# A two-block transformer kernel whose modulation sums move: from the third vector on, one multiply-and-add of VectorE per tile instead of column sums and transposes

## The reference, cut to what matters

```python
c_act = jax.nn.silu(c)                      # [1, 1024]
mod = c_act @ w_ada[l] + b_ada[l]           # w_ada: [1024, 6144]
sh1, sc1, g1, sh2, sc2, g2 = split(mod, 6)
h = rmsnorm(x, norm1_g) * (1.0 + sc1) + sh1
... attention and pooling of h, projected by w_out ...
x = x + g1 * mix
h2 = rmsnorm(x, norm2_g) * (1.0 + sc2) + sh2
x = x + g2 * conv_gated_ffn(h2, ...)
```

## Time and profile before

| | |
|---|---|
| median of 3 runs | 1458.22 us (1455.87 to 1458.29) |
| the profiled execution | 1456.54 us, of it a span of 1454.7 us |
| TensorE busy | 1401.7 us (96% of the span) |
| VectorE busy | 828.4 us (57%) |
| ScalarE busy | 649.5 us (45%) |
| GpSimd busy | 703.7 us (48%) |
| granted TensorE clock, mean | 0.985 of full speed |

### The profile page before, as it was taken

The page is one execution under the profiler, slowest core; times in us unless marked ns, Lnnn a source line. Parts: engine busy times, 40 slices in busy tenths (PEclk is TensorE's granted clock), DMA queues, the critical chain, the costliest instruction groups (busy, mean ns, idle before and its releaser), DMA issues.

```text
span 1454.7 us, 18428 instructions
## 1 busy us (share of the span) xinstructions
PE 1401.7 (96%) x7351; PEld 1181.1 (81%) x7351; DVE 828.4 (57%) x1289; ACT 649.5 (45%) x1199; POOL 703.7 (48%) x380
## 2 busy tenths in 40 slices
PE   7889989999999999999999999999999999999998
PEld 6668778988888888987778877788889888888886
DVE  5567746668888675656777976552357421302224
ACT  4455536444332331544776765456454331323231
POOL 1246554365555454554333454338815654545560
PEclk7799999999999999999999999999999999999999
DMA  8314523255555454321111211113211222232321
GB/s 320 141 65 161 175 103 114 102 209 172 187 198 201 177 202 153 124 87 59 59 59 59 87 59 58 59 58 134 98 59 59 87 87 87 90 113 88 111 92 58
DMA packets 32053, 167.59 MB, mean 115 GB/s; under 512 B 3552, under 2 KB 4192, under 8 KB 18912
## 3 DMA queue, kind: packets, MB, share of 16 engines
q1 hardware_dynamic: 31968, 166.42, 32.4%
HBM read 164.31 MB, written 2.10 MB: 114 GB/s over the span
## 4 chain that ended last, share of the span: by engine, by line
PE 84%; DVE 7%; ACT 4%; POOL 2%; issue 1%; DMA 1%; SPq 0%; DVEq 0%; ACTq 0%
PE B L552 81%; PE B L974 1%; POOL WL L2327 1%; ACT WH L1195 1%; DVE SC L1950 1%; PE B L784 1%; DVE SC L2178 1%; DMA RAW<-in_x 1%; DVE ZF L2153 1%; PE B L667 1%; POOL G L2365 0%; DVE M L2151 0%; DVE ZF L2133 0%; PE B L690 0%; DVE ZF L1861 0%
## 5 line engine op out<-in xcount | busy, mean ns | idle before, releaser
L2327 POOL TENSOR_TENSOR WL<-RAW,WH 128x512 fp32r<-128x512 f32 (+1 forms) x197 | 467.9, 2390 | 499.3 <-ACT WH L1195 453.7
L552 PE MATMUL B<-HH,WH 128*128 128x512 f32 (+2 forms) x1040 | 404.5, 391 | 5.9 <-ACT HH L1281 2.1
L552 PE MATMUL B<-HH,WL 128*128 128x512 f32 (+2 forms) x1040 | 397.2, 384 | 0.0
L552 PE MATMUL B<-HL,WH 128*128 128x512 f32 (+2 forms) x1040 | 385.8, 383 | 0.0
L1195 ACT ACTIVATE WH<-RAW 128x512 fp32r<-128x512 f32 (+1 forms) x197 | 191.8, 1004 | 178.8 <-PE B L552 164.0
L552 PEld LDWEIGHTS B<-HH,WH 128*128 128x128 f32 x1040 | 196.7, 189 | 45.9 <-issue 4.3
L552 PEld LDWEIGHTS B<-HH,WL 128*128 128x128 f32 x1040 | 196.6, 189 | 38.9
L552 PEld LDWEIGHTS B<-HL,WH 128*128 128x128 f32 x1040 | 191.7, 189 | 34.4
L552 PE MATMUL B<-ZR 128*128 128x256 f32 (+4 forms) x1048 | 151.2, 326 | 16.2 <-ACT SC L1536 3.4
L552 PE MATMUL B<-ZR,WH 128*128 128x512 f32 (+1 forms) x624 | 164.8, 353 | 0.1
L552 PEld LDWEIGHTS B<-ZR 128*128 128x128 f32 (+1 forms) x1048 | 120.0, 190 | 43.1 <-issue 14.6
(11 more groups left out here) (246 smaller groups left out, 1863.2 us busy)
## 6 DMA issues: line engine op xcount, KB each, us to landing
RAW<-in_slabs SPq DMA_DIRECT2D x102, 1024.0 KB, 4.9
ZF<-in_w_ada SPq DMA_DIRECT2D x84, 512.0 KB, 4.3
G<-in_w_ada SPq DMA_DIRECT2D x8, 512.0 KB, 10.2
RAW<-in_slabs SPq DMA_DIRECT2D x4, 768.0 KB, 4.5
RAW<-in_x SPq DMA_DIRECT2D x4, 512.0 KB, 7.5
SC<-in_w_ada SPq DMA_DIRECT2D x4, 512.0 KB, 9.7
out<-SC SPq DMA_DIRECT2D x8, 256.0 KB, 2.1
ROT<-in_consts SPq DMA_DIRECT2D x2, 512.0 KB, 6.1
```

Of the source, the lines that this page charges most:

```text
L552: return e.matmul(out, l, r, start=start, stop=stop)
L2327: e.tensor_tensor(lo[:, at], k.RAW[:, i % 2, at], hi[:, at].bitcast(F32), ALU.subtract).then_inc(*w.hit((i, q)))
```

## The change

On the host, `w_ada` and `w_ada_2` are transposed for the vectors 2 to 11. A tile (j, m) now has the output features 128m to 128m+127 on its partitions and the 1024 input features along the free dimension, 512 KB in one piece. c is wanted as a row on every partition: TensorE makes it once at the start (`c_rows`, 16 transposes into four banks of PSUM, after the sums of j = 1) and ScalarE copies it (four copies, after the first block's first norm) to `CR`, where the two accumulators were. One VectorE instruction per tile, `tensor_tensor_reduce`, multiplies the tile with the row, sums along it from the bias, and writes eight finished values per vector one column at a time. The chunks of j = 1 and 0 stay as they were.

The order changes too: after j = 1, 0 come 2, 4, 3, 5 and so on, one vector after another. In the attention loop tiles are taken at the steps 9, 11, ..., 31 and 32 to 35 (j = 2 and 4). All eight tiles of j = 3 stand at one point behind the loop, `("2", 0)`, ahead of the first residual. SyncE's load of slab 8, `("out", 3)`, goes from step 30 to behind the fourth of the loads that this point makes. The banks of PSUM are dealt out anew: `main` has two in the loop, and the ring `a` is gone.

```diff
-ADA = [(j, k) for j in (1, 0) for k in range(8)] + [(j, k) for k in range(8) for j in (4, 2)]
-ADA += [(j, k) for j in (3, 5, 6, 7, 8, 9, 10, 11) for k in range(8)]
+ADA = [(j, k) for j in (1, 0, 2, 4, 3, 5, 6, 7, 8, 9, 10, 11) for k in range(8)]
...
-    return j == 2 or j < 2 and k < SHARED
+    return j < 2 and k < SHARED
...
+ADA1 = [*range(9, 32, 2), *range(32, 36)]
...
-        many = {"1": 8 <= p < 32, "2": 0, "gate": 2, "val": 2, "down": 2 - point[1]}[g]
+        many = {"1": p in ADA1, "2": 8, "gate": 2, "val": 2, "down": 2 - point[1]}[g]
...
+        self.CR = [ZF[:, 3072:4096], ZF[:, 2048:3072]]
...
+    def c_rows():
+
+        pe.wait_ge(a_x["ca"])
+        for i in range(2):
+            for half in range(2):
+                b = B.take(pe, "main", ("c", i, half))
+                for q in range(4):
+                    m = 8 * i + 4 * half + q
+                    t = e.transpose(b[:, 128 * q:128 * q + 128], k.CA[:, m:m + 1].to_broadcast([128, 128]), k.IDN)
+                t.then_inc(*x_full.hit(("c", i, half)))
...
         ada_sum(j)
+        if j == 1:
+            c_rows()
...
-    B.deal(main=(0,), a=(1,), s=(2, 5, 3), t=(6, 7), o=(4,))
+    B.deal(main=(0, 1), s=(2, 5, 3), t=(6, 7), o=(4,))
...
-        for n in k.chunks["1", s]:
-            if by_pe(*ADA[n]):
-                ada_chunk(n, "a")
-        for j in k.sums["1", s]:
-            if j != 2:
-                ada_sum(j, ("t", "t"))
...
-    for j in k.sums["2", 0]:
-        ada_sum(j)
...
-                for j in k.sums[g, p]:
-                    ada_sum(j)
...
+    def ada_tile(n):
+
+        j, m = ADA[n]
+        i, _ = place(n)
+        src, c = k.early[i], (16 + 8 * j if j < 6 else 292 + 8 * (j - 6)) + m
+        dve.wait_ge(k.sig(f"in_ada{i}")[n])
+        dve.wait_ge(a_x["c", j // 6, 1])
+        e.tensor_tensor_reduce(out=src, in0=src, in1=k.CR[j // 6], scale=1.0, scalar=k.VT[:, c:c + 1], op0=ALU.mult, op1=ALU.add,
+                               accum_out=k.MOD[:, j, m:m + 1]).then_inc(*ada.hit((j, m)))
...
     def ada_point(point):
-        for j in k.sums.get(point, ()):
-            ada_mod(j)
         for n in k.chunks.get(point, ()):
-            if not by_pe(*ADA[n]):
-                ada_chunk(n)
+            ada_tile(n)
...
+    ada_point(("2", 0))
+
     def out_tile(m, half):
         residual(("mix", m) if half is None else ("mix", m, half), m, half, 2, ("x1", m, half))
-        if m == 3:
-            ada_point(("2", 0))
...
     for s in range(STEPS1):
-        if s in (0, 4, 12, 20, 30):
+        if s in (0, 4, 12, 20):
             weights()
...
+    for n in k.chunks["2", 0]:
+        ada(n + 2)
+        if n == k.chunks["2", 0][3]:
+            weights()
```

More of the change, by code:

```diff
@@ L120 @@
     tensor_scalar = scalar_tensor_tensor = tensor_reduce = tensor_tensor_scan = stream_shuffle = reciprocal = step
-    max = match_replace = dma_start = step
+    max = match_replace = dma_start = tensor_tensor_reduce = step
 class Banks:
@@ L348, in ada_plan @@
 def ada_plan():
-    points = [("1", s) for s in range(STEPS1)] + [("2", p) for p in range(4)]
+    points = [("1", s) for s in range(STEPS1)] + [("2", 0)]
     for i, what in enumerate(("u0", "u1", "d0", "u2", "d1", "d2")):
@@ L722, in pe_program @@
     QKS = qk_sets(k)
-    B.deal(main=(5, 6, 7, 0, 1, 2, 3, 4))
+    B.deal(main=(3, 1, 2, 0, 4, 5, 6, 7))
     first_slab("q0k", ("q0", "k"), 0)
@@ L825, in pe_program @@
         if 32 <= s < 36:
-            mix(s - 32, 0, 4, ("main", "a", "s", "s")[s - 32])
+            mix(s - 32, 0, 4, ("main", "main", "s", "s")[s - 32])
         if s > 35:
@@ L1281, in act_program @@
         e.activation(k.HH[:, j, :], k.slot(j), ACT.Identity, bias=k.MOD[:, 0, j:j + 1]).then_inc(*hh.hit((0, j)))
+    for i in range(2):
+        for half in range(2):
+            act.wait_ge(x_full["c", i, half])
+            act.wait_ge(ada_full["sum", 1 - i, 1])
+            e.activation(k.CR[i][:, 512 * half:512 * half + 512], B["c", i, half][:, :], ACT.Copy).then_inc(
+                *xs.hit(("c", i, half)))
+            B.free(("c", i, half), xs["c", i, half])
     QKS = qk_sets(k)
@@ L1851, in ada_chunk @@
         i, _ = place(n)
-        dst, src, c = k.ACC[j % 2], k.early[i], k.CA[:, 8 * (j // 6) + kt:8 * (j // 6) + kt + 1]
+        dst, src, c = k.ACC[j % 2], k.early[i], k.CA[:, kt:kt + 1]
         dve.wait_ge(k.sig(f"in_ada{i}")[n])
-        if kt == (SHARED if j < 2 else 0):
+        if kt == SHARED:
             dve.wait_ge(a_x["ca"])
-            if j > 2:
-                dve.wait_ge(ada_full["sum", {3: 1, 4: 0}.get(j, j - 2), 1])
             e.tensor_scalar(dst, src, c, None, ALU.mult).then_inc(*ada.hit((j, kt)))
@@ L1861, in ada_chunk @@
             e.scalar_tensor_tensor(out=dst, in0=src, scalar=c, in1=dst, op0=ALU.mult, op1=ALU.add).then_inc(*ada.hit((j, kt)))
-    def ada_mod(j):
[L1864 to L1869, removed]
+    def ada_tile(n):
[6 more added lines that the diff above has]
+                               accum_out=k.MOD[:, j, m:m + 1]).then_inc(*ada.hit((j, m)))
+        if m == 7:
+            ada.also(("mod", j))
+    def ada_mod(j):
         for half in range(2):
@@ L2621 @@
         args[name] = nc.dram_tensor(f"in_{name}", arr.shape, _mybir.dt.from_np(arr.dtype), kind="ExternalInput").ap()
+    sums = {n: _np.asarray(inputs[n][0]) for n in ("w_ada", "w_ada_2")}
+    arrays["in_w_ada"] = _np.ascontiguousarray(sums["w_ada"][:, 0:2048])
+    arrays["in_w_ada_rows"] = _np.ascontiguousarray(_np.concatenate([sums["w_ada"].T, sums["w_ada_2"].T]))
+    for name in ("w_ada", "w_ada_rows"):
+        args[name] = nc.dram_tensor(f"in_{name}", arrays[f"in_{name}"].shape, _mybir.dt.float32, kind="ExternalInput").ap()
     arrays["in_slabs"] = packed({n: _np.asarray(inputs[n]) for n in _SLABS})
```

38 lines of the change are left out of this document (15 added, 23 removed).

## The result

| | before | after |
|---|---|---|
| median | 1457.64 us (4 runs, 1455.87 to 1458.29) | 1446.41 us (4 runs, 1446.04 to 1446.52) |
| the profiled execution | 1456.54 us, span 1454.7 | 1446.43 us, span 1444.6 |
| granted TensorE clock, mean | 0.985 | 0.984 |

The kernel is faster: ratio 0.9918, 95% interval 0.9905 to 0.9931, 11.2 us by the medians and 10.1 by the two profiled executions. Predicted were 1446.4 us and -11.8. One execution of experiment 6 took 2756.77 us, a slow one, and is left out of its figures.

The account below looks back on a forecast made before the run. TensorE was taken to bound the loop and feed-forward, GpSimd the loop's end, VectorE and ScalarE behind the first residual. -14.2 + 0.3 - 1.5 - 0.9 + 10.6 - 6.1 = -11.8 us, giving 1446.4 us; range 1436 to 1459.

Parts of the forecast that it names:

- Start, 0: At the start, 16 TensorE transposes and four ScalarE copies for the row of c fit in: 0 us.
- Loop, -14.2 + 0.3: Attention loop: eight chunks of 1.78 us leave TensorE, -14.2 us; one unit waits a few tenths for softmax, +0.3.
- the unit of steps 8 and 9: Attention-loop unit with little else to do, the only one expected to wait for softmax: +0.3 us.
- neither closes up: Attention loop: VectorE keeps its number of large instructions up to step 23 and transfers are halved, so neither becomes limiting.
- the second rival: Softmax or GpSimd paces the loop: -7 instead of -14, no gain at the loop's end, 1455 us; chance 0.14.
- A tile, 1.4: Price of one new VectorE tile instruction: 1.4 us, between 1.28 and 3.0.
- the half-rate rival: VectorE's tile runs at half rate, 3.0 us, and the kernel ends slower: 1469.5 us; chance 0.12.
- End of the loop, -1.5 and -0.9: Loop's end: fewer VectorE hold-ups of GpSimd, -1.5 us (0 to 3); TensorE's sum of j = 4 goes, -0.9.
- The batch, +10.6: Behind the loop: eight j = 3 tiles, paced by loads in pairs, make the first residual 10.6 us late.
- Feed-forward, -6.1: First block's feed-forward: seven vectors each lose 0.87 us of TensorE in a stretch it fills, -6.1 us.
- the third rival: Tile at half rate, 3.0 us: 1.6 us more a tile costs 23.1 us, giving 1469.5 us; chance 0.12.
- +12 in all: Feed-forward with 3.0 us tiles: VectorE busy 260 of 280 us, too much where products and tiles meet, +12 us.

Follow-up runs that it names:

- experiment 6: Changed kernel with the 16 tiles of j = 2 and 4 at steps 8 to 23, none from there to the loop's end: 1448.28 us, ratio 0.9942.
- experiment 12: Kernel before the change with only the 16 transposes for the row of c added at the start: 1458.37 us, ratio 1.0004.
- experiment 1: Changed kernel with eight unused TensorE matmuls per unit put back in the attention loop: 1459.79 us, ratio 1.0019.
- Experiment 5: Changed kernel with the tiles of j = 3 moved into the loop's last steps and slab 8 loaded at step 33: 1440.76 us, ratio 0.9882.
- the second kernel of 7 and 8: Changed kernel, j = 2 and 4 at steps 8 to 23, j = 3 at 31 to 38, slab 8 loaded at 33, split right behind slab 7: 1442.60 us.
- Experiment 3: Changed kernel without the loads of the last six j = 3 tiles, which reread the two buffers: 1442.80 us, ratio 0.9897.
- experiment 2: Changed kernel with eight unread TensorE transposes per vector 5 to 11 put back in the feed-forward: 1453.60 us, ratio 0.997.
- Experiment 11: Changed kernel with every one of the 80 tile instructions issued twice: 1546.07 us, ratio 1.0601.

## Why the prediction was right

**Start, 0.** Right to what the runs can tell (experiment 12). ScalarE's four copies take 2.02 us, the split of slab 1 starts at 51.99 behind them, its low part is done at 58.6, and the product that wants it starts at 59.60, no later than before.

**Loop, -14.2 + 0.3.** The mechanism is right and shown from both sides: it came with the change and went with experiment 1. The size was -11.9, and the units tell where the 2 us are. From one unit's transposes to the next one's (L784, then L795) seven intervals of the loop each had a chunk, and they are shorter by 1.54 to 1.73, 1.66 in the mean, where 1.78 was taken as the length of a chunk: 0.9 in eight. Ahead of them TensorE now waits once for ScalarE's exponential, 1.29 us at 112.32, where the first chunk stood before. That is the place that the prediction named with the unit of steps 8 and 9, at +0.3; what waits there are the scores of a later unit, for a bank that the exponential frees. TensorE has no other wait between 104 and 158 us. So "neither closes up" held behind this place, and the second rival was wrong. Of the signs that were named, the stretch was to be 13 to 14 us shorter and came short of it, and the wait for the exponential, a sign against the forecast, came this once.

**A tile, 1.4.** Measured 1.36, or 1.21 from start to start; the half-rate rival was wrong for this instruction.

**End of the loop, -1.5 and -0.9.** The first measured -2.2, and experiments 5 and 6 move it by +3.7 and -2.5 with more and with fewer tiles. The second did not come: the transposes of j = 4 are gone, but the stretch is 0.7 longer. What eats it is TensorE's clock. Two windows of 6 us, each right behind the last low part, of before and then of after:

```profile
197.00:203.00 6.00, 5.67 (x29) 4.81 (x30) 1.46 (x3) 0.00 (x0) 0.27 (x1) 1.00 0.95 350
```

```profile
182.00:188.00 6.00, 6.00 (x20) 4.78 (x21) 3.53 (x6) 0.00 (x0) 0.00 (x0) 0.72 0.60 194
```

TensorE had waited for GpSimd in both, 0.93 us before and 2.40 in after; in after its granted clock is 0.72 in this window, which is 0.28 x 6 = 1.7 us of work at the full level, about the 1.6 that are missing. The experiments bear this out. The same 51 matmuls stand behind the last low part in after and in experiment 6, where that part ends at 184.99; they take 10.9 and 9.3 us. Experiment 6 keeps the full clock there, while after has 0.87 in the window of 182 to 195 us:

```profile
182.00:195.00 13.00, 11.77 (x65) 9.96 (x64) 1.29 (x2) 2.06 (x5) 2.92 (x3) 1.00 0.00 0
```

There, and in the second kernel of 7 and 8, which keeps it as well, the whole stretch to the last product is 10.5 us, which is 11.39 less the predicted 0.9. What makes the clock fall in one and not in the other is open: TensorE waits 1.2 us ahead of it in experiment 6, but 2.5 in the second kernel of 7 and 8.

**The batch, +10.6.** Measured +9.7, by the shape that was forecast: pairs of tiles, a load of 4.0 to 4.1 between them, 19.9 us from the gain of the norm to the residual against the 20.8 that were worked out. (Less the 10.1 available that is 10.7, where the prediction has 10.6.) Experiment 5 gives 9.7 back. Experiment 3 corrects the picture at one point: the loads are only half of it, 5.1 us. Without them more of the tiles meet GpSimd's low parts, five instead of three, which the loads had spread out of their way. That nothing behind the residual absorbs the lateness held too (-0.1).

**Feed-forward, -6.1.** -6.3, and +6.3 back with experiment 2. By the end of the block both are 5.5, since 0.8 is given back at the last residuals.

**The sum.** The terms give -10.1 in the profiled executions where -11.8 stood: the loop gave 2.0 less, the sum of j = 4 1.6 less, the stretch to the end 1.3 less (0.8 of it the last residuals of the first block, the rest the second block, where no instruction differs and no experiment went), and the start, the tail, the batch and the feed-forward gave 3.2 more. The median came out at the predicted 1446.4 because the median of before lay 1.1 to 1.7 above its profiled execution and that of after did not; the closeness to a tenth is luck, the terms are right to within about 2 us each, and the misses went both ways.

**What was wrong** is the third rival's price. It put 23.1 us on 1.6 us more a tile, and said that gain turns to loss at a tile of about 2.2. Experiment 11 had 1.3 us more a tile and lost 99.7. The step that failed is "+12 in all" for the feed-forward, worked out from busy time (260 of 280 us): neither the turns with GpSimd's 4.6 us instructions nor the chain from VectorE over ScalarE and GpSimd back to TensorE was in it. Where the gain would end is not measured; if the loss grew evenly with the tile, the 11 us would be used up by 0.15 us more a tile (an estimate from 99.7 us for 1.3 us). So this rival had the direction right and its size far too small.

## What to carry to other kernels

Work taken from the engine that is full is worth nearly what it lasts: 11.9 of 14.2 us in the loop, 5.5 of 6.1 in the feed-forward. What it costs on the engine that receives it depends on the place: the same eight instructions cost 9.7 us in one piece ahead of a residual, and 3.7 at the loop's end, where they stand beside GpSimd. Look for the place where a finished operand is first needed, and spread its work and loads before that: this alone was 5.7 us, and together with an earlier split 9.0. Don't read spare time off a busy share: in the feed-forward VectorE had 110 us free, and 72 us more work cost 83.

## What the runs showed of the hardware

- A VectorE instruction with two SBUF sources and a GpSimd instruction of about the same length alternated one by one when both had a list of them: 2.30 and 2.24 us each in place of 1.28 and 1.27 (experiment 3). Beside GpSimd's low part of 128x2048, 4.6 us by itself, one tile took 5.55 us (experiment 11).
- The multiply-and-add that sums along the row costs no more than one that does not: 1286 ns against 1283, plus 78 ns.
- TensorE work that starts 1.5 us earlier can end only 0.4 us earlier (the 24 matmuls from 102.46 are done at 106.5, from 103.94 before at 106.9): the granted clock was 0.50 from 104 to 107 us, where before it was 1.00, after the same wait of 2.2 us (experiment 12).
- The same 51 matmuls behind the last low part took 10.9 us where the granted clock was 0.72 over the first 6 us, and 9.3 where it was 1.00 (after, experiment 6).
